# Expert stage of a hybrid decoder step: the last gate and up columns as one product, and other PSUM banks for the down products and the transposes

## The reference

```
def swiglu(h, w_gate, w_up, w_down):
    return (jax.nn.silu(h @ w_gate) * (h @ w_up)) @ w_down

def moe_swiglu(h, router_w, w_gate, w_up, w_down):
    ...
    for e in range(N_EXPERTS):
        out = out + combine[..., e:e + 1] * swiglu(h, w_gate[e], w_up[e], w_down[e])
    return out
```

## Time and profile before

| | us |
|---|---|
| three runs, median | 1635.34 |
| lowest and highest of them | 1633.65, 1636.84 |
| profiled execution | 1640.97 |
| its span in the trace | 1639.3 |
| expert stage: an expert's row transposes to the next one's, fourth expert (1113.55 to 1208.77) | 95.2 |

### The profile page before, as it was taken

How to read it: one execution, slowest core, us unless ns; L and a number is a source line. 1 busy time by engine, 2 the same in 40 slices (tenths; PEclk the granted TensorE clock), 3 DMA queues, 4 the chain that set the end, 5 groups by cost and what they waited for, 6 DMA issues and landing times.

```text
span 1639.3 us, 25518 instructions
## 1 busy us (share of the span) xinstructions
PE 1578.3 (96%) x8912; PEld 1399.8 (85%) x8913; DVE 1168.0 (71%) x1499; ACT 1000.7 (61%) x1188; POOL 84.1 (5%) x100
## 2 busy tenths in 40 slices
PE   8999999999999999999969999999999999999993
PEld 8889999999999978998958888888888888888782
DVE  6667437644444578634649989898998989899894
ACT  5663234444433675324547788888788887878772
POOL 3000110000000000120000000000000001000000
PEclk9999989999999999989979999999999999999997
DMA  7434444454445333443449999999999999999994
GB/s 238 135 102 141 141 141 124 129 153 145 147 142 160 116 116 109 133 142 116 142 151 367 367 368 376 374 375 371 379 366 365 381 372 371 366 379 368 357 363 151
DMA packets 223038, 399.10 MB, mean 243 GB/s; under 512 B 12336, under 2 KB 103520, under 8 KB 222960
## 3 DMA queue, kind: packets, MB, share of 16 engines
q1 hardware_dynamic: 215920, 372.84, 65.6%
q0 software_dynamic: 6544, 23.37, 5.3%
q10 hardware_dynamic: 496, 1.84, 0.3%
HBM read 383.84 MB, written 14.16 MB: 243 GB/s over the span
## 4 chain that ended last, share of the span: by engine, by line
PE 77%; DVE 7%; ACT 6%; DMA 5%; issue 4%; ACTq 0%; DVEq 0%; POOL 0%; POOLq 0%; SPq 0%
PE bank L1475 10%; PE bank L1477 10%; PE bank L1476 10%; PE bank L1799 8%; PE bank L1801 8%; PE bank L1800 8%; PE bank L1791 4%; PE bank L1790 4%; PE bank L1792 4%; DMA weights_raw<-in_moe_w_up 3%; ACT weights_high L688 2%; DVE weights_low L1361 2%; DMA weights_raw<-in_moe_w_down 1%; PE bank L1633 1%; PE bank L1683 1%
## 5 line engine op out<-in xcount | busy, mean ns | idle before, releaser
L1361 DVE TENSOR_TENSOR weights_low<-weights_raw,weights_high 128x1024 fp32r<-128x1024 f32 x522 | 621.4, 1220 | 77.2 <-ACT weights_high L914 65.7
L914 ACT ACTIVATE weights_high<-weights_raw 128x1024 fp32r<-128x1024 f32 x522 | 549.0, 1060 | 145.3 <-DMA weights_raw<-in_moe_w_up 63.0
L977 DVE TENSOR_TENSOR weights_low<-weights_raw,weights_high 128x1024 fp32r<-128x1024 f32 (+1 forms) x186 | 224.6, 1213 | 297.1 <-ACT weights_high L688 297.0
L688 ACT ACTIVATE weights_high<-weights_raw 128x1024 fp32r<-128x1024 f32 (+1 forms) x186 | 193.6, 1045 | 250.6 <-PE bank L1477 241.1
L1475 PE MATMUL bank<-moving_high,weights_high 128*128 128x320 f32 x944 | 301.2, 319 | 0.7 <-DVE moving_low L1051 0.7
L1476 PE MATMUL bank<-moving_low,weights_high 128*128 128x320 f32 x944 | 297.2, 315 | 0.0
L1477 PE MATMUL bank<-moving_high,weights_low 128*128 128x320 f32 x944 | 297.0, 315 | 0.0
L1799 PE MATMUL bank<-weights_high,expert_in_high 128*128 128x512 f32 (+1 forms) x768 | 290.0, 378 | 2.6 <-DVE weights_low L1361 1.9
L1801 PE MATMUL bank<-weights_high,expert_in_low 128*128 128x512 f32 (+1 forms) x768 | 286.0, 372 | 0.0
L1800 PE MATMUL bank<-weights_low,expert_in_high 128*128 128x512 f32 (+1 forms) x768 | 285.9, 372 | 0.0
L1475 PEld LDWEIGHTS bank<-moving_high,weights_high 128*128 128x128 f32 x944 | 182.7, 194 | 4.0 <-DVE moving_low L1051 1.6
(11 more groups left out here) (301 smaller groups left out, 1804.2 us busy)
## 6 DMA issues: line engine op xcount, KB each, us to landing
weights_raw<-in_moe_w_gate SPq DMA_DIRECT2D x176, 512.0 KB, 5.5
weights_raw<-in_moe_w_up SPq DMA_DIRECT2D x176, 512.0 KB, 5.7
weights_raw<-in_moe_w_down SPq DMA_DIRECT2D x176, 512.0 KB, 5.3
weights_raw<-in_w_in SPq DMA_DIRECT2D x80, 512.0 KB, 3.6
weights_raw<-in_dense_w_gate SPq DMA_DIRECT2D x22, 512.0 KB, 3.8
weights_raw<-in_dense_w_up SPq DMA_DIRECT2D x22, 512.0 KB, 3.7
weights_raw<-in_w_out SPq DMA_DIRECT2D x16, 512.0 KB, 3.4
weights_raw<-in_dense_w_down SPq DMA_DIRECT2D x16, 512.0 KB, 3.4
```

The source lines that it names most:

```text
L688: fn(whi[:, p % RING, 0:n], raw[:, p % RING, 0:n], ACT.Copy).then_inc(high_done, 1)
L914: fn(whi[:, p % RING, 0:n], raw[:, p % RING, 0:n], ACT.Copy).then_inc(high_done, 1)
L1361: v.tensor_tensor(wlo[:, p % RING, 0:n], raw[:, p % RING, 0:n], whi[:, p % RING, 0:n].bitcast(F), ALU.subtract).then_inc(low_done, 1)
```

## The change

The last group (j = 5) is no longer two sets of products of 256 columns. PE skips the gate chunk, and in the up chunk runs one set of 512 columns: the moving operand takes 256 columns from a gate piece's slot and 256 from the up piece's slot two pieces later, and both results lie side by side in bank 4. The first half takes pieces 40 and 42, the second 41 and 43; `pe_mark` counts one up after the first half and three after the second. Since gate and up now end together, ACT's silu of the last group moves from the gate chunk to the up chunk. The down products go to banks 2 and 3, the transposes of `He` to banks 6 and 7, the row-finding product to bank 5; PE waits for the emptying of the last item's down results (`y_ready`) also before the gate columns of group 1, which write bank 2.

```diff
-    DOWN_BANK = 6
+    DOWN_BANK, SLOT_BANK, TURN_BANK, END_BANK = 2, 5, 6, 4
...
+    END = 2 * closing[("gate", NG - 1)]
+    END_COLS = groups[-1][1]
+    END_SLOTS = [sorted(((END + h2) % RING, (END + 2 + h2) % RING)) for h2 in range(2)]
...
+    def gate_tile(j):
+        return bank[2 * (j % 2)][:] if j < NG - 1 else bank[END_BANK][:, END_GATE]
...
-            if kind == "gate" and closed:
+            if closed and (kind == "gate" and j < NG - 1 or kind == "up" and j == NG - 1):
                 act.wait_ge(pe_mark, 2 * NEC * item + (MB + 2 * i + 2))
...
-                ins = nc.tensor.transpose(bank[4 + j % 2][:, 128 * n:128 * n + 128], He[:, 128 * t:128 * t + 128], ident[:])
+                ins = nc.tensor.transpose(bank[TURN_BANK + j % 2][:, 128 * n:128 * n + 128], He[:, 128 * t:128 * t + 128], ident[:])
...
+            if j == 1 and kind == "gate" and part == 0:
+                pe.wait_ge(y_ready, 2 * item + NO)
+            if kind == "gate" and j == NG - 1:
+                return
             for half in range(2):
                 p = 2 * i + half
+                if kind == "up" and j == NG - 1:
+                    pe.wait_ge(low_done, 2 * NEC * item + (2 * NDENSE + p + 1))
+                    if half == 0 and ahead:
+                        pe.wait_ge(idx_ready, item + 2)
+                    b = bank[END_BANK][:].rearrange("p (s n) -> p s n", s=2)
+                    s0_, s1_ = END_SLOTS[half]
+                    for q in range(KD // 2):
+                        kk = half * (KD // 2) + q
+                        w = slice(q * cols, (q + 1) * cols)
+                        mm(b, xeh[:, kk, :], whi[:, s0_:s1_ + 1:s1_ - s0_, w], start=kk == 0, stop=False)
+                        mm(b, xeh[:, kk, :], wlo[:, s0_:s1_ + 1:s1_ - s0_, w], start=False, stop=False)
+                        ins = mm(b, xel[:, kk, :], whi[:, s0_:s1_ + 1:s1_ - s0_, w], start=False, stop=kk == KD - 1)
+                    ins.then_inc(pe_mark, 1 + 2 * half)
+                    continue
```

More of the change, by code:

```diff
@@ L426, in hybrid_trunk_program, with up_tile @@
     NO = len(OUTS)
+    END = 2 * closing[("gate", NG - 1)]
+    END_COLS = groups[-1][1]
+    END_SLOTS = [sorted(((END + h2) % RING, (END + 2 + h2) % RING)) for h2 in range(2)]
+    assert len({(a == (END + h2) % RING) for h2, (a, b) in enumerate(END_SLOTS)}) == 1
+    assert len(groups) == 6 and 2 * END_COLS == 512 and closing[("up", NG - 1)] == END // 2 + 1
+    END_GATE, END_UP = slice(0, END_COLS), slice(END_COLS, 2 * END_COLS)
+    if END_SLOTS[0][0] != END % RING:
+        END_GATE, END_UP = END_UP, END_GATE
     def width(i):
         return ECH[i % NEC][4] * ECH[i % NEC][6]
+    def gate_tile(j):
+        return bank[2 * (j % 2)][:] if j < NG - 1 else bank[END_BANK][:, END_GATE]
+    def up_tile(j):
+        return bank[1 + 2 * (j % 2)][:] if j < NG - 1 else bank[END_BANK][:, END_UP]
     def group_tiles(j):
@@ L906, in hidden_high @@
             act.wait_ge(het_psum, NG * item + j + 1)
-            fn(heh[:, ts[0]:ts[-1] + 1, :], bank[4 + j % 2][:, 0:128 * len(ts)], ACT.Copy).then_inc(heh_ready, 1)
+            fn(heh[:, ts[0]:ts[-1] + 1, :], bank[TURN_BANK + j % 2][:, 0:128 * len(ts)], ACT.Copy).then_inc(heh_ready, 1)
         def high_of(item, i, half):
@@ L925, in chunk @@
                     act.wait_ge(he_ready, NG * item + (j - 1))
-                fn(sge[:, j % 2, 0:cols], bank[2 * (j % 2)][:, 0:cols], ACT.Silu).then_inc(gate_emptied, 1)
+                fn(sge[:, j % 2, 0:cols], gate_tile(j), ACT.Silu).then_inc(gate_emptied, 1)
             if i + AHEAD < last:
@@ L1332, in rows_of_slots @@
                 dve.wait_ge(kept, item)
-            v.tensor_copy(gate[:], bank[DOWN_BANK][:, 1:2])
-            v.tensor_tensor(idx[:], bank[DOWN_BANK][:, 0:1], own_row[:], ALU.add).then_inc(idx_ready, 1)
+            v.tensor_copy(gate[:], bank[SLOT_BANK][:, 1:2])
+            v.tensor_tensor(idx[:], bank[SLOT_BANK][:, 0:1], own_row[:], ALU.add).then_inc(idx_ready, 1)
         def keep_rows(item):
@@ L1352, in hidden_low @@
             dve.wait_ge(heh_ready, NG * item + j + 1)
-            v.tensor_tensor(hel[:, ts[0]:ts[-1] + 1, :].rearrange("p k s -> p (k s)"), bank[4 + j % 2][:, 0:128 * len(ts)],
+            v.tensor_tensor(hel[:, ts[0]:ts[-1] + 1, :].rearrange("p k s -> p (k s)"), bank[TURN_BANK + j % 2][:, 0:128 * len(ts)],
                             heh[:, ts[0]:ts[-1] + 1, :].rearrange("p k s -> p (k s)").bitcast(F),
@@ L1372, in chunk @@
                 dve.wait_ge(gate_emptied, NG * item + (j + 1))
-                v.tensor_tensor(He[:, c0:c0 + cols], bank[1 + 2 * (j % 2)][:, 0:cols], sge[:, j % 2, 0:cols],
+                v.tensor_tensor(He[:, c0:c0 + cols], up_tile(j), sge[:, j % 2, 0:cols],
                                 ALU.mult).then_inc(he_ready, 1)
@@ L1746, in rows_of_slots @@
             for t, (_, sz) in enumerate(TOK):
-                ins = mm(bank[DOWN_BANK][:, 0:2], pick[0:sz, t, :], pair[0:sz, t, :], start=t == 0, stop=t == NT - 1)
+                ins = mm(bank[SLOT_BANK][:, 0:2], pick[0:sz, t, :], pair[0:sz, t, :], start=t == 0, stop=t == NT - 1)
             ins.then_inc(idx_psum, 1)
```

## The result

The changed kernel takes 1643.39 us (median, 1641.33 to 1645.90) where the kernel before takes 1635.34: a ratio of 1.0052, 95% interval 1.0032 to 1.0072. Measured once more, beside other runs, it took 1642.79, ratio 1.0050 (1.0031 to 1.0070). The forecast was no change at 1636.0 with a range to 1643.0; of its rivals, B comes nearest: PE waits for piece 42 in every expert.

A forecast was written before the change was run, and what follows sets the result against it. PE was taken to set the pace, with the loop of slots (transfer, ACT, DVE, PE) just fast enough. Merge -2.4, wait +1.0 and late release +2.1 gave +0.7: 1636.0 us, range 1626.0 to 1643.0.

The forecast's parts named there:

- B: Rival, chance 0.28: PE's first half waits for low 42 in every expert; 1642.3, or 1639.8 with part recovered.
- The merged products, -2.4: Last group on PE: 24 products of 512 columns at 0.227 us save 0.3 us an expert, -2.4 us in eight.
- rival C: Merged products on PE: two-place moving operand takes 0.240 us a product, nothing saved, +3.1, 1638.4; chance 0.08.
- Down's step, 0: Down products in banks 2 and 3: step stays 0.2335 us, so no gain taken; -6.9 kept as a rival.
- rival A: Down products: banks 6 and 7 cause the 0.2335 step, so 0.227 now; 1626.0, or 1629.1 with waits; chance 0.28.
- Waits that cost nothing: Emptied down results before group 1, row-finding product and later silu: ample margin, no cost taken.
- The wait, +1.0: PE before the merged products, for piece 42: one wait paid, then lead stays; 1.0 us, from 0 to 2.7.
- The late release, +2.1: Piece 41's slot comes free only after the second half, delaying piece 47: 0.3 us an expert, seven experts, +2.1.
- Part of the 0.7 disappears: Transfer of piece 53, 0.6 to 0.7 us late, finds the queue still filled; 0.3 taken, bounds 0 and 0.7.
- What would show it: Profile signs: product steps, PE's wait (over 1.3 us each expert for B), piece 47's start, row-transpose distances (over 96 for B).

The follow-up runs named there:

- the run in turn with the wait: Changed kernel with last group's pieces loaded gate, up, gate, up, each half releasing its own two, PE still waiting for low 42 first; 1638.03 us, ratio 1.0009.
- the run with only the banks: Kernel before with only the banks moved (down in 2 and 3, transposes in 6 and 7), last group's 256-column products unmerged; 1635.46 us, ratio 0.9995.
- the run with only the wait: Kernel before, but PE waits for low 42 before piece 40 and low 43 before piece 41; 1641.16 us, ratio 1.0024.
- the run where PE does not wait: Changed kernel with pieces loaded gate, up, gate, up, no wait for piece 42, but piece 41's slot still released late; 1635.45 us, ratio 1.0003.
- the run in turn: Changed kernel with last group's pieces loaded gate, up, gate, up; first half needs 40 and 41, each half releases its own two; 1635.85 us, ratio 0.9987.

## Why the prediction was wrong

The terms of the sum, as the runs have them: merge -2.4 (profile), wait +3.9, release +6.7. Merge and wait together are +1.5, and the run in turn with the wait, which has just these two, shows +1.5 (-0.5 to +3.6); with some 2 us of uncertainty on either side, so close an agreement is partly luck. The release is the difference between that run and the changed kernel beside it, 8.2 - 1.5, so that all three add up to 8.2 is no further evidence; what bears the 6.7 out is the 0.8 us an expert in DVE's rows and the 0.7 in the row transposes.

- *The merged products, -2.4*: right, 0.30 us an expert, and rival C is out: two stretches of 256 columns run at 0.227 us. The Trainium skill ("TensorE: Matmul & The Clock Gate", section "Back-to-back issue gap") gives the formula with 2.5 ns, by which 0.06 us an expert is an estimate, for a product by itself, and says that a stream with a weight load before each product is spaced otherwise. This kernel has such a stream (8913 weight loads for 8912 products before), and its measured 0.30 us decides.
- *Down's step, 0*: right. It is 0.233 in banks 2 and 3 too, and rival A is out. Whether it is the change of bank after three products was not tried.
- *Waits that cost nothing*: right as far as the run with only the banks can tell.
- *The wait, +1.0*: here the prediction failed. Its step "the conversions and transfers behind it are not delayed as much, so at the next expert they stand that much better against PE. One wait ... is paid and then stays" does not hold: in the run with only the wait the conversions stand six slots ahead in the down part and follow PE's releases, 33.76 to 33.78 us in each of six experts. The lead can't grow beyond the six slots; from there on a wait delays the loop as much as PE, and the next expert pays again. Some lead was regained, so the step was not wrong altogether, but the regained lead ends at the full ring, and the prediction took it to be as long as the greatest lag. The rows ahead gave a hint of it: the lag of piece 42 was there, 0.96, 1.34 and 1.47 us in the second to fourth experts (the 1.34 in the earlier trace rows), while PE ran at 95.23 us an expert; how much of it would return they did not show. In the changed kernel the late release keeps the conversions from filling the ring (9 of ACT's waits are for a down product there, 66 with the early release), and PE's wait comes back each time, 0.63 to 1.69 us in the experts two to eight. For the forecast's +1.0 once, the wait alone measured +3.9 (1.5 to 6.2) over the eight.
- *The late release, +2.1*: the mechanism was right and the size was off. "Part of the 0.7 disappears" in the transfers' queue was wrong once the wait had made the loop the bound: all of 0.8 us in eight experts counts, +6.7. In the run where PE does not wait, no cost can be told. One reading was wrong besides: slot 42 does not come free in mid-group. `pe_mark` is a count, and it goes up by one after the first half, so only slot 40 is released there, and 41, 42 and 43 at the end.
- *The two together*: they were summed as if independent. The release shows a cost only behind the wait. Rival B had the place right, and named the release as the other way there ("or the late release costs the whole 0.7"). That its 1642.3 is only 1 us off is luck: it is made of 9.4 for the wait and nothing for the release, where the runs show 3.9 and 6.7. The range ended 0.4 us below what came.
- *What would show it*: three signs pointed at B, as written: a wait in each expert (though 0.63 to 1.69 us, 8.0 us in seven, and not over 1.3 each time), ACT's piece 47 right behind the second half, and 96.5 to 98.0 us between row transposes.

## What to carry to other kernels

A lead in a ring can be no longer than the ring. A consumer that asks for its pieces earlier than it did pays for it again in each turn of the loop, less what lead the ring had left, and slots given back later cost most when it waits already; the question is then whether the producers have spare time within one turn, not over the whole. Merge products from pieces that arrive next to each other, as in the run in turn, and look for the other work of the producer's engines that stands in the same stretch.

## What was not expected of the hardware

In the changed kernel's second profile, PE waited 1.82 us in the fourth expert, and then the granted clock fell to half (the stretch of the wait, the next 3 us, then 3 us more).

```profile
1189.70:1191.70 2.00, 0.18 (x3) 0.03 (x1) 1.64 (x2) 1.65 (x2) 0.00 (x0) 1.00 0.98 379
1191.90:1194.90 3.00, 3.00 (x8) 2.34 (x8) 2.96 (x4) 2.60 (x3) 0.00 (x0) 0.51 0.96 362
1195.00:1198.00 3.00, 3.00 (x14) 2.46 (x13) 2.22 (x3) 1.06 (x1) 0.00 (x0) 0.94 0.95 350
```

PE's rows from the end of the wait:

```profile
1191.67 0.57 PE L1808 MATMUL bank<-weights_high,expert_in_high 128*128 128x512 f32 x1 [1.82 <-DVE weights_low L1376]
1192.04 0.63 PE L1809 MATMUL bank<-weights_low,expert_in_high 128*128 128x512 f32 x1
1192.47 0.63 PE L1810 MATMUL bank<-weights_high,expert_in_low 128*128 128x512 f32 x1
1192.89 0.63 PE L1808 MATMUL bank<-weights_high,expert_in_high 128*128 128x512 f32 x1
```

Some seven products came 0.427 us apart, the 1.2 GHz level, and not 0.227: 7 x 0.2 = 1.4 us on top of the wait. The same followed two of the waits in front of the row-finding product, those of 1.41 us (shown above) and 1.57 us. It did not follow every one: after the wait of 1.69 us shown above the granted clock stayed at 1.00. The prediction had counted on 1.00 throughout, from pauses that were shorter one by one.
